# Moving the modulation tiles in SyncE's load queue: each unit's tiles go behind the weights of the sixth unit past it

## The reference

```python
proj = h @ w_in[layer]                                    # first block: projection of the mixer
...
mod = (jax.nn.silu(c) @ w_ada[l] + b_ada[l]).reshape(b, N_SUB, 3, D_MODEL)   # second block: 1024 x 9216
```

## Time and profile before

| | |
|---|---|
| median of 3 runs | 2940.36 us (2938.63 to 2943.82) |
| the profiled execution's own time | 2931.5 us |
| its span | 2930.2 us |
| PE busy | 2707.9 us (92%) |
| POOL busy | 1270.0 us (43%) |
| ACT busy | 931.4 us (32%) |
| DVE busy | 868.3 us (30%) |
| the stretch of the change (chunks 0 to 7) | 378.1 to 587.1 us |

### The profile page before, as it was taken

How to read it: one execution, slowest core, us unless ns; L and a number is a source line. 1 busy time by engine, 2 the same in 40 slices (tenths; PEclk the granted TensorE clock), 3 DMA queues, 4 the chain that set the end, 5 groups by cost and what they waited for, 6 DMA issues and landing times.

```text
span 2930.2 us, 30093 instructions
## 1 busy us (share of the span) xinstructions
PE 2707.9 (92%) x12126; PEld 2159.6 (74%) x12126; DVE 868.3 (30%) x1425; ACT 931.4 (32%) x1497; POOL 1270.0 (43%) x645
## 2 busy tenths in 40 slices
PE   8999999975699899999999999998977699899998
PEld 7888878744466688788888788887855487788886
DVE  4222146543666311322211311102026423311101
ACT  4233211202455422332322322223246423322221
POOL 4444434412477344444444444444433344444443
PEclk9999999976799999999999999998989799899999
DMA  4222257712000122222322223231210022132321
GB/s 157 95 99 90 90 206 281 267 40 73 7 1 1 65 94 94 87 94 94 100 93 95 79 94 97 91 96 62 94 49 1 6 96 86 52 100 95 98 92 61
DMA packets 75754, 261.48 MB, mean 89 GB/s; under 512 B 9184, under 2 KB 10464, under 8 KB 75616
## 3 DMA queue, kind: packets, MB, share of 16 engines
q1 hardware_dynamic: 72368, 255.45, 26.3%
q10 hardware_dynamic: 3248, 4.12, 0.5%
HBM read 257.44 MB, written 2.10 MB: 89 GB/s over the span
## 4 chain that ended last, share of the span: by engine, by line
PE 66%; DVE 4%; POOL 3%; ACT 2%; issue 1%; DMA 0%; ACTq 0%; POOLq 0%; DVEq 0%
PE ps L243 57%; POOL prob L1419 2%; PE ps L254 1%; PE ps L1218 1%; PE ps L1575 1%; PE ps L1188 1%; PE ps L1175 1%; PE ps L1176 0%; PE ps L1540 0%; PE ps L279 0%; POOL prob_d L1866 0%; PE ps L1564 0%; ACT hs L431 0%; PE ps L1225 0%; PE ps L1541 0%
## 5 line engine op out<-in xcount | busy, mean ns | idle before, releaser
L230 POOL TENSOR_TENSOR split_ring<-raw_ring,split_ring 128x1024 fp32r<-128x1024 f32 x416 | 1006.2, 2422 | 1301.8 <-ACT split_ring L223 1301.7
L243 PE MATMUL ps<-hs,split_ring 128*128 128x512 f32 x6240 | 1439.6, 392 | 34.8 <-DVE hs L333 8.9
L243 PEld LDWEIGHTS ps<-hs,split_ring 128*128 128x128 f32 x6240 | 1179.9, 189 | 293.4 <-issue 14.7
L223 ACT ACTIVATE split_ring<-raw_ring 128x1024 fp32r<-128x1024 f32 x416 | 437.2, 1052 | 559.6 <-PE ps L243 393.0
L243 PE MATMUL ps<-ffn_act,split_ring 128*128 128x512 f32 x2112 | 495.4, 396 | 0.0
L243 PEld LDWEIGHTS ps<-ffn_act,split_ring 128*128 128x128 f32 x2112 | 397.8, 188 | 97.0
L512 ACT ACTIVATE ffn_act<-tmp 128x512 fp32r<-128x512 f32 x88 | 55.6, 632 | 385.2 <-DVE tmp L548 385.2
L1419 POOL TENSOR_SCALAR prob<-prob,small 128x512 f32<-128x512 f32 (+3 forms) x128 | 140.4, 1115 | 59.7 <-DVE small L1463 59.7
L548 DVE TENSOR_TENSOR tmp<-ps,tmp 128x512 f32<-128x512 f32 x44 | 30.4, 691 | 380.6 <-PE ps L243 380.6
L243 PE MATMUL ps<-split_ring,hs 128*128 128x512 f32 (+1 forms) x480 | 106.1, 384 | 10.3 <-POOLq L196 7.9
L243 PEld LDWEIGHTS ps<-split_ring,hs 128*128 128x128 f32 x480 | 88.9, 197 | 26.5 <-POOLq L196 8.1
(11 more groups left out here) (294 smaller groups left out, 2451.7 us busy)
## 6 DMA issues: line engine op xcount, KB each, us to landing
raw_ring<-in_wstream SPq DMA_DIRECT2D x380, 512.0 KB, 3.4
ada_w<-in_w_ada SPq DMA_DIRECT2D x64, 576.0 KB, 5.8
raw_ring<-in_wstream SPq DMA_DIRECT2D x32, 384.0 KB, 3.0
x<-in_x_t SPq DMA_DIRECT2D x4, 512.0 KB, 6.6
decay<-in_decay ACTq DMA_DIRECT2D x4, 512.0 KB, 3.6
out_t<-x SPq DMA_DIRECT2D x8, 256.0 KB, 2.0
raw_ring<-in_wstream SPq DMA_DIRECT2D x4, 304.0 KB, 5.8
cos_r<-in_cos_r ACTq DMA_DIRECT2D x1, 256.0 KB, 3.6
```

Of the source, the lines that this page charges most:

```text
L223: nc.scalar.activation(self.split[:, s, 0, :], self.raw[:, s, :], ACT.Copy).then_inc(self.sem("unit_hi"), 1)
L230: nc.gpsimd.tensor_tensor(self.split[:, s, 1, :], self.raw[:, s, :], self.split[:, s, 0, :].bitcast(F32), ALU.subtract).then_inc(self.sem( ...
L243: mm = self.nc.tensor.matmul(out, lhs, rhs, start=first and j == 0, stop=last and j == 2)
```

## The change

The order of SP's queue alone. All units of the four stages from `a.in.fm` to `a.cmp` are issued in one list, and behind unit i (for i from 6 to 37) stand the tiles that belong to unit i - 6. `ADA_TILES` is as before: three tiles, three, two, none. So chunk c's tiles 0 to 2 stand behind unit 4c + 6, tiles 3 to 5 behind unit 4c + 7, tiles 6 and 7 behind unit 4c + 8. The waits in front of each load, the buffers, and the programs of PE, DVE, ACT and POOL are the same.

```diff
-    def sp_ada_stage(self, name, chunk0):
-        for t in range(self.plan[name]["n"]):
-            for u in range(4):
-                self.sp_unit(name, t, u)
-                if u > 1:
-                    self.sp_ada(chunk0 + t, u - 2)
-            for u in (2, 3):
-                self.sp_ada(chunk0 + t, u)
+    ADA_STAGES = ("a.in.fm", "a.in.vg", "a.in.vr", "a.cmp")
+    ADA_BEHIND = 6
+
+    def sp_ada_stages(self):
+
+        units = [(name, t, u) for name in self.ADA_STAGES for t in range(self.plan[name]["n"])
+                 for u in range(len(self.plan[name]["widths"]))]
+        for i, (name, t, u) in enumerate(units):
+            self.sp_unit(name, t, u)
+            if self.ADA_BEHIND <= i < self.ADA_BEHIND + 4 * 8:
+                self.sp_ada((i - self.ADA_BEHIND) // 4, (i - self.ADA_BEHIND) % 4)
...
             if name == "a.in.fm":
-                self.sp_ada_stage(name, 0)
-            elif name == "a.in.vg":
-                self.sp_ada_stage(name, 5)
-            elif name == "a.in.vr":
-                self.sp_ada_stage(name, 6)
-            else:
+                self.sp_ada_stages()
+            elif name not in self.ADA_STAGES:
                 self.sp_stage(name)
```

## The result

The changed kernel takes 2953.12 us (median of 5 runs, 2951.27 to 2954.08) against 2939.44 us for the kernel before (median of 5, 2934.67 to 2943.82): ratio 1.0046, 95% interval 1.0031 to 1.006, so 13.7 us slower. The profiled execution has a span of 2950.0 us, against 2930.2 before; that is 19.8 us and more than the medians differ, because the profiled execution of before was a short one (2931.5 us by its own time, under all the timed runs shown). The trace can place the time, but its total is some 6 us too large.

A forecast was written before the change was run, and what follows sets the result against it. PE, busy 92%, bounds the kernel, waiting at chunk 0's `pe_ada` and two meets. Terms -2.9 - 3.7 + 8.4 + 1.0 + 3.7 + 2.5 = +9.0 us gave 2949.4 us, range 2937 to 2961.

The forecast's parts named there:

- The gain at the meets: PE's pauses before vg and vr, ended by POOL's drain, shrink: 3.76 to 0.9 us (-2.9) and 4.19 to 0.5 (-3.7).
- The cost in chunks 1 to 4: DVE and POOL hold each other up, so PE waits 2.1 us for each chunk's sum: 4 x 2.1 = +8.4 us.
- The walk: One chunk followed from PE's unit 0: three splits among DVE's tiles, tile 7 ends at 23.9 us, PE wants it at 21.8.
- Chunk 0: A further POOL split between tiles 6 and 7 costs +1.9 us; half may come back from low clock: +1.0, bounds 0 and +4.
- Chunk 5: In vg, tile 3 lands near 9.8 us and tiles 3 to 7 with two splits end at 19.6: +3.7, bounds +1 and +6.
- The clock: Low clock behind the new waits of chunks 1 to 3, 0 to 1.7 us each: +2.5, bounds 0 and +5.
- The tables of retention: PE waits for these tables, issued behind the meet as before: 0, at best -0.5 us.
- vr's chunk: The low clock at vr's first unit (7.4 instead of 5.44 us) stays: 0, or -1.9 if not.
- Rival A: Same mechanism but weaker: wait 1 us instead of 2.1, no clock loss; +2, about 2942, no measurable change. Chance 0.22.
- Rival B: Faster: meets' gain stays, DVE meets tile 7's deadline in chunks 1 to 4; -10.9, or -3 with chunk 5 late. Chance 0.13.

The follow-up runs named there:

- the fastest run: The changed kernel with tiles one unit further forward, DVE adding tiles in front of evictions, and the running sum in PSUM from chunk 1 on: 2913.57 us, ratio 0.9918.
- the memset run: The changed kernel, but for units 3 to 34 POOL fills the low part with zeros instead of subtracting: 2925.63 us, ratio 0.9966.

## Why the prediction was right, and where it was off

The direction and the mechanism held. The time, forecast 2949.4 us, is 2953.1, inside the range. But the change was forecast +9.0 us and is +13.7, and the stretch that the sum is about grew by 17.4 us in the profiles: the terms below were short by nearly half, and that the medians moved less than the profiles was luck for the number. By the steps:

- *The gain at the meets* (-2.9, -3.7): 3.76 became 0.83 and 4.19 became 0.31, so -2.9 and -3.9.
- *The cost in chunks 1 to 4* (4 x 2.1): 2.06, 2.07, 2.07 and 2.91, in all 9.1. The walk was right to 0.1 us in three of four, since all its durations were rows; in chunk 4 it lacked 0.46 us that DVE pauses in front of tile 4, over half of the 0.8. That pause is no effect of the change, for it stands at the same place before (at 501.68). That it is the port and neither the tiles nor SP is shown from both sides: tiles a unit earlier change nothing, and one SBUF input less, with POOL's work the same, removes it.
- *Chunk 0* (+1.0): the wait grew by 1.9 us, as walked; the low clock behind it gave back 0.2 instead of 0.9.
- *Chunk 5* (+3.7): the sum comes 21.9 us behind the stage's start, +5.9. Tile 3 landed at 10.45 us (walked: 9.8). The five additions from there took 11.38 us, with two whole splits among them. The mechanism was right and the sum was not: from 9.8 us, five additions of 1.52 us and two splits of 2.2 end at 21.8 and not at 19.6 us, so one of the two splits that the prediction names was left out. Added up rightly the term is +5.9, as measured, and the forecast 2951.6.
- *The clock* (+2.5): this term is the most mis-sized. The chunks behind the sums of 1, 2 and 3 took 23.64, 23.47 and 24.67 us instead of 22.04, in all +5.7, beyond my bound of 5; and the one-column passes themselves became longer, 4.00 instead of 2.06 us in chunk 5 and 0.1 to 0.7 in chunks 1 to 4, +3.2, which I had not in the sum at all. The windows (columns as in the earlier trace rows) show it behind the pauses of chunks 1 to 3:

```profile
444.81:452.17 7.36, 7.36 (x27) 5.93 (x27) 0.17 (x1) 0.00 (x0) 0.12 (x1) 0.77 0.70 274
472.73:479.91 7.18, 7.18 (x26) 5.84 (x27) 0.17 (x1) 0.00 (x0) 0.00 (x0) 0.79 0.68 267
500.85:509.24 8.39, 8.39 (x26) 6.70 (x27) 0.17 (x2) 0.00 (x0) 0.00 (x0) 0.66 0.44 171
```

- *The tables of retention* (0, at best -0.5): the wait for them went from 5.60 to 4.26 us, -1.3.

The terms measured: -2.9 - 3.9 + 9.1 + 1.7 + 5.9 + 5.7 + 3.2 - 1.3 - 0.2 (vr's chunk) = +17.3, and the stretch is 17.4 us longer. The medians differ by 13.7; the rest of the program and the lead before the stretch add 2.4 us in the two profiles, and the spread of single executions covers the difference. I can't say which part of the 17.3 was smaller in the timed runs.

Rival A (the wait halves, the clock stays) fell: the pauses are 2.06 us and each had its low clock. Rival B named the right deadline: when DVE's additions come 5.4 us earlier or run at their own length, the waits go. But removing the port conflict alone did not bring its 11 us, since vg's landing of tile 3 took its place: the run with the sum in PSUM is 4.1 us below the kernel before, near the -3 that the rival gave for a late chunk 5.

## What to carry to other kernels

In this kernel the even order cost 13.7 us. Before you smooth a bursty engine, see what the bursts avoid: here POOL's burst lay where DVE had nothing to do, and the even order put three splits of four into DVE's busiest time, against a deadline with 1.6 us of slack. An accumulation like this one, which VectorE does beside GpSimd's subtractions, gains by keeping one of its two inputs in PSUM where the two overlap (17.8 us on the new queue, 2.3 on the old), and work with a deadline should stand in front of work that can wait, as the evictions here can. And where a stage has two limits close behind each other, an experiment that lifts one of them shows only the distance to the second.

## What the runs showed of the hardware that was not expected

- A pause of 2.07 us in front of 2 us of one-column passes brought the clock down every time (granted clock 0.66 to 0.79 in the next 7 to 8 us), where a pause of 1.41 us in front of wide matmuls did not the earlier trace rows. One-column passes alone, as in the chunks without a pause, did not either. But the pause need not be long: 0.57 us behind the passes of chunk 2, in the run with the sum in PSUM on the old queue, was followed by 7.26 us at 0.76, and the second meet's 0.31 us in the fastest run by 7.23 us at 0.76. Nor does its length decide alone: behind the first meet's 0.83 us, where no pause stood in front of the passes, vg's matmuls took 13.56 us in two runs (granted clock 1.00 in the new queue's run with the sum in PSUM) and 15.1 us in four (0.72 in the first 6 us of the fastest run).
- An addition of 128x1152 with its sum in PSUM takes the same 1.42 us as in SBUF, though PSUM is read and written; the first tile's tensor_scalar takes 1.41 us into PSUM and 0.81 into SBUF.
- POOL's memset, which reads nothing, did not hold up DVE's additions: with two SBUF inputs each, none of 56 took over 1.421 us, and 18 of them began while a memset ran. The Trainium skill (SBUF — State Buffer, "SBUF: two separate sides") says that a VectorE instruction with two SBUF inputs contends only with a GpSimd instruction that reads SBUF; the memset run agrees. The first tile's tensor_scalar is another matter. In that run no memset was under way when one started, and the five memsets that came during one took 1.14 us (four) and 1.43 us instead of 0.95, and ended 0.89 us behind its end. POOL was the one held up, and whether a memset can hold up a first tile no run shows. Chunk 2, DVE, then POOL:

```profile
444.54 0.81 DVE L822 TENSOR_SCALAR ada_acc<-ada_w,c_silu 128x1152 f32<-128x1152 f32 x1
...
445.11 1.14 POOL L231 MEMSET split_ring<- 128x1024 f32 x1 [6.53 <-ACT split_ring L223]
```
